# Hybrid attention trunk: six first-mixer runs per stage, and another engine for the fifth turned blocks

## What is computed

```
# mixer A: 8 heads, each 64-token chunk sees itself and 8 chunks before
sc = einsum('bqhd,bkhd->bhqk', qc, kc) * scale + bias ; p = softmax(sc)
out = einsum('bhqk,bkhd->bqhd', p, vc)
# mixer B: 8 query heads over 2 key heads, window of 2 chunks, a sink logit per head
m = max(max(sc), sink); p = exp(sc - m); p = p / (sum(p) + exp(sink - m))
gates = sigmoid(h @ w_gate + b_gate)
x = x + (g_a * (a @ w_branch_a) + g_b * (b @ w_branch_b)) @ w_out
```

## Time and profile before

| | us |
|---|---|
| median of 3 runs | 2589.5 (2589.29 to 2591.73) |
| the profiled execution | 2588.69 |
| its span on the core | 2586.9 |
| TensorE matmul busy | 2557.4 (99%) |
| VectorE busy | 1823.0 (70%) |
| ScalarE busy | 1038.8 (40%) |
| GpSimd busy | 286.4 (11%) |

### The profile page before, as it was taken

How to read it: one execution, slowest core, us unless ns; L and a number is a source line. 1 busy time by engine, 2 the same in 40 slices (tenths; PEclk the granted TensorE clock), 3 DMA queues, 4 the chain that set the end, 5 groups by cost and what they waited for, 6 DMA issues and landing times. The chain is left out here.

```text
span 2586.9 us, 35453 instructions
## 1 busy us (share of the span) xinstructions
PE 2557.4 (99%) x12822; PEld 2095.1 (81%) x12822; DVE 1823.0 (70%) x3321; ACT 1038.8 (40%) x2035; POOL 286.4 (11%) x442
## 2 busy tenths in 40 slices
PE   8999999999999999999999999999999999999998
PEld 6888777888888888888778887778888888888886
DVE  8766555644888777768996665555459777776687
ACT  6222466522533333344542225664235333333444
POOL 0000232344000000000000002224430000000000
PEclk9999999999999999999999999999999999999999
DMA  4323543453133233395423345425422233225843
GB/s 149 130 102 114 176 140 118 135 178 115 60 116 109 90 107 122 99 280 162 151 102 117 111 136 160 145 84 179 151 106 92 88 106 118 91 97 169 260 117 126
DMA packets 200332, 336.92 MB, mean 130 GB/s; under 512 B 18672, under 2 KB 79968, under 8 KB 200160
## 3 DMA queue, kind: packets, MB, share of 16 engines
q1 hardware_dynamic: 191936, 311.47, 36.5%
q10 hardware_dynamic: 8224, 23.20, 2.6%
HBM read 240.76 MB, written 92.92 MB: 129 GB/s over the span
## 5 line engine op out<-in xcount | busy, mean ns | idle before, releaser
L1407 PE MATMUL ps<-op_hi,up_hi 128*128 128x512 f32 x1232 | 479.9, 389 | 2.5 <-DVE third_sum L2996 2.5
L1409 PE MATMUL ps<-op_hi,up_lo 128*128 128x512 f32 x1232 | 479.3, 389 | 0.0
L1408 PE MATMUL ps<-op_lo,up_hi 128*128 128x512 f32 x1232 | 479.3, 389 | 0.0
L1407 PE MATMUL ps<-in_hi,up_hi 128*128 128x512 f32 x728 | 285.0, 392 | 2.6 <-DVE up_lo L2491 2.1
L1408 PE MATMUL ps<-in_lo,up_hi 128*128 128x512 f32 x728 | 283.7, 390 | 0.0
L1409 PE MATMUL ps<-in_hi,up_lo 128*128 128x512 f32 x728 | 283.7, 390 | 0.0
L1407 PEld LDWEIGHTS ps<-op_hi,up_hi 128*128 128x128 f32 x1232 | 231.3, 188 | 51.0 <-issue 3.3
L1409 PEld LDWEIGHTS ps<-op_hi,up_lo 128*128 128x128 f32 x1232 | 231.3, 188 | 48.2
L1408 PEld LDWEIGHTS ps<-op_lo,up_hi 128*128 128x128 f32 x1232 | 231.3, 188 | 47.8
L2091 ACT ACTIVATE up_hi<-up_raw 128x512 fp32r<-128x512 f32 x252 | 158.1, 630 | 278.5 <-PE ps L1409 271.6
L1360 POOL CAST w_hi<-w_raw 128x256 fp32r<-128x256 f32 x184 | 81.5, 485 | 1468.0 <-DMA w_raw<-w_lin 1209.9
(11 more groups left out here) (255 smaller groups left out, 4758.1 us busy)
## 6 DMA issues: line engine op xcount, KB each, us to landing
up_raw<-w_gu SPq DMA_DIRECT2D x42, 1024.0 KB, 5.1
act_raw<-ff_saved SPq DMA_DIRECT2D x154, 256.0 KB, 2.8
w_quarter<-w_lin SPq DMA_DIRECT2D x52, 512.0 KB, 4.5
w_raw<-w_lin SPq DMA_DIRECT2D x48, 512.0 KB, 4.2
ff_saved<-ff_block SPq DMA_DIRECT2D x88, 256.0 KB, 2.0
ff_saved<-ff_mix SPq DMA_DIRECT2D x66, 256.0 KB, 2.0
gated<-gates_saved SPq DMA_DIRECT2D x32, 512.0 KB, 4.2
dn<-w_dn_a SPq DMA_DIRECT2D x48, 256.0 KB, 4.0
```

Source lines behind the costliest of these rows:

```text
L1407: pe.matmul(out, w1, x1, start=first, stop=False, skip_group_check=True)
L1408: pe.matmul(out, w1, x0, start=False, stop=False, skip_group_check=True)
L1409: return pe.matmul(out, w0, x1, start=False, stop=last, skip_group_check=True)
```

## The change

Mixer A's pairs 0 to 3 are taken in the order 0, 3, 1, 2 (`A_ORDER`) and make two runs of four units: 0 with 3, 1 with 2, each of 640 key columns per head. With pairs 4 to 7 there are six runs in a stage. In each, four blocks per head go through `t_ps` and a fifth through bank 7. ScalarE copies only the four; VectorE copies the fifth (`take_fifth`), at the last unit of the next run, and TensorE's value transposes and its next fifth blocks wait for that (`fifth_ready`). Mixer B's heads now lie in one bank, and are copied once the whole run is weighed. The inverse transposes move to later runs. The fill of a stage stays 24 steps in the first group and 10 in the others, in other portions.

```diff
+A_ORDER = (0, 3, 1, 2, 4, 5, 6, 7)
 def run_start(u):
-    return u & (~7 if unit(u)[0] == "B" else ~3 if u % PHASE < 4 else ~1)
+    return u & (~7 if unit(u)[0] == "B" else ~3 if u % PHASE < PHASE // 2 else ~1)
-FILL_A = ((8, 0, 4, 4, 2, 2, 2, 2),) + ((2, 0, 3, 2, 1, 1, 1, 0),) * (GROUPS - 1)
+FILL_A = ((8, 0, 6, 0, 4, 2, 2, 2),) + ((3, 0, 3, 0, 1, 1, 1, 1),) * (GROUPS - 1)
...
             def turn_values(L, s, c):
-                if last_wide(run_start(s) - 1) is not None:
-                    pe.wait_ge(turned_ready, L * TURNS + turned_through(last_wide(run_start(s) - 1)))
+                if last_full(run_start(s) - 1) is not None:
+                    pe.wait_ge(fifth_ready, L * FIFTHS + fifths_through(run_start(s) - 1))
...
             def turn_run(L, last):
+                if fifths > 0:
+                    pe.wait_ge(fifth_ready, fifths)
+                pe.wait_ge(v_ready, L * VALUES + values_before(last + 1))
+                final = key_blocks(mixer, unit(first)[3]) - 1
+                for e in range(2):
+                    mm = pe.transpose(last_ps[:, e * P:(e + 1) * P], soft(first + e)[:, final * P:(final + 1) * P], ident[:, :])
+                mm.then_inc(turned, 1)
...
             def take_turned(L, last):
-                if wide(last):
-                    act.wait_ge(turned, made + 3)
-                    act.activation(probs_t[:, :, HALF:A_COLS], last_ps.rearrange("p (e n) -> p e n", e=2),
-                                   ACT.Copy).then_inc(turned_ready, 1)
...
+            def take_fifth(L, last):
+                dve.wait_ge(turned, L * TURNS + turned_through(last))
+                taken = L * HEAD_PAIRS + weighed_through(last + 1)
+                if taken > 0:
+                    dve.wait_ge(head_done, taken)
+                dve.tensor_copy(probs_t[:, :, HALF:A_COLS], last_ps.rearrange("p (e n) -> p e n", e=2)).then_inc(fifth_ready, 1)
...
                         for u in weighed_in(s - 1):
                             take_heads(L, u)
+                    if s < UNITS and s == run_end(s) and s > run_end(0) and unit(run_start(s) - 1)[0] == "A":
+                        take_fifth(L, run_start(s) - 1)
```

More of the change, by code:

```diff
@@ L305, in quarters_at @@
 def quarters_at(s, afters):
-    return [2 * eight + j for j, after in enumerate(afters) for eight in inverses_at(s, after)]
+    return sorted(2 * eight + j for j, after in enumerate(afters) for eight in inverses_at(s, after))
 def inverses_before(u):
@@ L327, in turned_through, with copied_through, fifths_through, last_full @@
 def turned_through(u):
[L329 removed]
+    runs = {run_start(v): 3 if unit(v)[0] == "A" else 2 for v in range(u + 1)}
     return sum(runs.values())
+def copied_through(u):
+    return 2 * len({run_start(v) for v in range(u + 1)})
+def fifths_through(u):
+    return len({run_start(v) for v in range(u + 1) if unit(v)[0] == "A"})
 def scores_through(u):
     return u + 1 + sum(wide(v) for v in range(0, u + 1, 2))
[L337 to L338 removed]
+def last_full(u):
+    return max((v for v in range(u + 1) if unit(v)[0] == "A"), default=None)
+def block_place(p):
+    return A_BLOCKS - 1 - p if p < 2 else 0
 HEAD_PAIRS = UNITS // 2
@@ L637, in o_ps @@
         def o_ps(u):
-            mixer, _, _, p = unit(u)
-            if mixer == "A":
-                return bank(6)[:, P if p == 1 else 0:2 * P if p == 1 else P]
+            if u < LAST_UNIT - EIGHT:
+                place = (u - run_start(u)) // 2
+                return bank(6)[:, place * P:(place + 1) * P]
+            p = unit(u)[3]
             return bank(4 if p % 4 < 2 else 6)[:, p % 2 * P:(p % 2 + 1) * P]
@@ L681, in turned_to @@
         def turned_to(u):
-            if unit(u)[0] == "A":
-                return probs_t[:, u % 2, P if u % PHASE in (2, 3) else 0:]
+            mixer, _, e, p = unit(u)
+            if mixer == "A":
+                return probs_t[:, e, block_place(p) * P:]
             return probs_t[:, u % EIGHT // 4, u % 4 * P:(u % 4 + 1) * P]
@@ L1966, in take_turned @@
                     return
-                cols = 3 * P if last - first == 3 else min(key_blocks(mixer, p) * P, HALF)
                 for e in range(2):
@@ L2010, in split_o @@
                     if j == XK:
-                        act.wait_ge(gates_past, L + 1)
+                        act.wait_ge(gate_done, (L + 1) * GATE_HALVES - 1)
                     act.activation(o_hi[j][:, :], x_sb[:, j, :], ACT.Copy).then_inc(o_hi_ready, 1)
@@ L2813, in scale_last @@
                 dve.wait_ge(inverse_step, L * (EIGHTS + 1) + EIGHTS)
-                own = inverse[:, stats_of(EIGHTS - 1)].rearrange("p (r i o) -> p i r o", i=4, o=1)
-                for i in range(4):
-                    both = probs[(i + 2) % NPROBS][:, 3 * P:5 * P].rearrange("p (r n) -> p r n", r=2)
-                    op = dve.tensor_tensor(both, own[:, i, :, :].to_broadcast([P, 2, P]), both, ALU.mult)
+                own = inverse[:, stats_of(EIGHTS - 1)].rearrange("p (r e o) -> p e r o", e=2, o=1)
+                for e in range(2):
+                    both = probs[2 + e][:, 0:HALF].rearrange("p (r n) -> p r n", n=P)
+                    op = dve.tensor_tensor(both, own[:, e, :, :].to_broadcast([P, HALF // P, P]), both, ALU.mult)
                 op.then_inc(inverse_step, 1)
```

101 lines of the change are left out of this document (51 added, 50 removed).

## The result

| | before | after |
|---|---|---|
| median, us | 2589.4 (2587.4 to 2591.7) | 2616.3 (2615.2 to 2620.3) |
| the profiled execution | 2588.69 | 2620.32 |
| its span | 2586.9 | 2618.5 |

The change makes the kernel slower: ratio 1.0107, 95% interval 1.0091 to 1.0123. 2605.7 was predicted, with a range of 2597 to 2612, so the sign was right and the size too small by 10.6 us on the median. Against its own base the sum of the prediction gave 2604.9 for the profiled execution, which took 2620.3: 15.4 us are missing.

A forecast was written before the change was run, and what follows sets the result against it. TensorE was taken as the bound, busy 193.94 of 194.00 us in the first layer's attention. Terms -4.8 + 8.8 + 8.4 + 3.8 = +16.2 took 2588.7 to 2604.9, or 2605.7 for the median; range 2597 to 2612.

The forecast's parts named there:

- The run that goes: Mixer A stages: one run fewer saves 0.6 us in each of eight stages, minus 4.8 (4.0 to 5.2).
- The crossings: Gate tile halves changing within a fill, eight times: TensorE waits for VectorE's bank 0 read, 1.1 each, plus 8.8.
- The value turns: First group's second and third runs, each layer: turns wait for VectorE's fifth copy, holes 3.2 and 1.0, plus 8.4.
- The scores: Groups two to four, behind mixer A's second run: scores wait for VectorE's maxima, 0.6 six times, plus 3.8 us.
- rival (1): Clock falls to 1.2 GHz in the 3.2 hole at the value turns: +4.3 per layer, 2614 us; chance 0.10.
- The inverse turns and the DMAs and GpSimd products behind them move by one or two runs within their group: In the attention, these move within their group, the last two staying where they were; no cost in the sum.
- near 4.3 of 4.5: In one-step runs VectorE's maxima, inverse, heads, fifth and rotary step take near 4.3 of 4.5 us; nobody waits.

The follow-up runs named there:

- best: Changed kernel with two inverse buffers, fills outside the gate's half changes, ScalarE's copy of the fifth block, value turns two filling steps later: 2585.6 us (0.9985).
- best_dve: As best, but VectorE keeps the copy of the fifth block, behind the run's second maximum: 2584.5 us (0.9981).
- b_cross: Kernel before with fill portions 3, 3, 2, 1, 1, 0, 0 in groups two to four, making six crossings: 2596.1 us against 2590.0 (1.0024).
- double: Changed kernel with two buffers for the turned inverses, so VectorE's copy waits for the save before the last one: 2609.1 us (1.0073).
- early1: Changed kernel, still one inverse buffer, with SyncE's saves of the inverses two places earlier, ahead of the swapped loads: 2612.0 us (1.0084).
- b_inverse: Kernel before, seven runs, with the inverse transposes moved to the runs where the change has them: 2602.0 us against 2590.0 (1.0048).

## Why the prediction was right and wrong

- **The run that goes: right.** -4.8 by the pieces, less 0.8, since the scores of pairs 1 and 2 take 1.38. `best` and `best_dve`, where nearly every wait is gone, are 4.6 and 5.7 below before, 3.3 of it in the attentions, where these two terms make 4.0.
- **The crossings: right.** 1.1 each in the trace, 1.0 each in `b_cross`. Eight of them were forecast at 8.8 and took 8.8. The price came from the earlier trace rows and a like wait elsewhere.
- **The value turns: right.** 8.1 for 8.4; VectorE's copy took 0.42 for my 0.40.
- **The scores: right in place and sum, 3.3 for 3.8, with some luck.** I had 0.6 in each of three groups; they are 0.9, 0.3 and 0.4. A rotary step takes 1.13 in the second group where I had counted 0.61, others less.
- **The clock: a rival (1) that came true on top of the forecast.** I gave it 0.10 because the hole of the earlier trace rows had not done it, in one execution; in eight of the other profiled executions that same hole did. It cost 4.1 in the profiled execution, where the rival said 8.6. The Trainium skill (TensorE: Matmul & The Clock Gate, Why this matters for your kernels) warns of idle gaps between bursts. The attentions' traces agree for all but one of the gaps of 2.5 us or more; at 1.9 to 2.4 some executions have the lower clock behind the gap and some have not. I had reckoned the hole at 3.2 myself, longer than any in the trace, and 0.10 was too little for a case without a row.
- **The failed step: "The inverse turns and the DMAs and GpSimd products behind them move by one or two runs within their group".** It was put at nothing, without a price: I had looked at who uses an inverse, not at who may make the next one. The take of an inverse waits for the save of the one before (one buffer), the save stands in SyncE's list behind loads that wait for a rotary step, and the heads' copies that TensorE needs stand behind the take. Three turns in three successive runs put this chain on the path: +8.9, and +2.8 of low clock behind it. `double`, `early1` and `b_inverse` each show it from another side. The step "near 4.3 of 4.5" for VectorE in these runs was also no reason for calm: it counted work and not waits.
- **The range** was built from the bounds of the terms that I had, which add up to 2611 (2611.8 with the gain's own bound of 4.0 in place of 4.8); the missing one is as large as the largest of these.

Open: how much low clock follows a hole. The fill of six steps behind the hole of 3.1 took 5.1 us in one layer of the changed kernel and 6.7 in the other, 5.8 and 5.7 in `double`, 4.3 being reckoned and 4.2 measured without the low clock. And why the save of 4 KB took 4.0 us. The rows show a load of 512 KB ahead of it in the same queue, here and in the kernel before, where a save behind it was read back after 4.2 us and one without it after 1.8. That the load is the cause was not tried.

## What to carry to other kernels

When a step moves, follow not only those who need its result but the buffer that it writes: who must have emptied it, in which queue that stands, and what stands in front of it there. Price a wait with everything queued behind it on its own engine, and ask of an edit that frees time what else bounds the stage: here the same edit was worth 12 us with two buffers and less with one (1.6 by the medians, 8.8 in the attentions of one execution). With the copy's place early enough and its consumer behind two steps of other work, no wait for the copy was left, with either engine. And do not conclude from one execution that a hole of a given length leaves the clock alone.

## What the runs showed of the hardware

- Holes of TensorE of 2.5 to 4.5 us in the attentions were followed by its lower clock (matmuls of 512 columns 0.43 apart instead of 0.23) in all places but one. Of those of 1.9 to 2.4 us some were and some were not: the same hole of 2.1 us in the same place of the program in eight profiled executions of fourteen, one of 1.9 in five. What followed a hole cost 1.3 to 2.8 us in the changed kernel.
- Handing a PSUM bank of 128 x 512 fp32 from TensorE to VectorE and back costs 1.27 us from the last matmul's start to the next one's: 0.44, 0.69 for the read, 0.14.
- A save of 4 KB can hold an engine for over 4 us (4.0 from its issue here, with 512 KB ahead of it in the queue). Before, the reads of a saved inverse followed its save by 1.8 us (the save at 349.45, the first of them at 351.27), and by 4.2 where the same 512 KB stood ahead (361.30 and 365.51); whether these waited for the save alone is not shown.
